# A hybrid encoder step on one core: closing sums taken place by place, and the first expert's token numbers, splits and tables in another order

## What is computed

```python
def _layer(...):
    ...
    h = _layer_norm(alpha * x + mix, ln1_g, ln1_b)
    moe_out = _moe(h.reshape(B * L, D_MODEL), w_router, b_router, w_gu, b_gu, w_down, b_down)
    y = _layer_norm(alpha * h + moe_out, ln2_g, ln2_b)

def _moe(x2, ...):
    logits = jnp.dot(x2, w_router) + b_router
    top_val, top_idx = lax.top_k(logits, TOP_K)          # 4 of 32
    gates = jax.nn.softmax(top_val, axis=-1)
    ...
    gu = jnp.dot(xb, w_gu[e]) + b_gu[e]                  # rows of one expert, 1024 x 2048
    gate, up = jnp.minimum(gu[:, :1024], 7.0), jnp.clip(gu[:, 1024:], -7.0, 7.0)
    hmid = gate * jax.nn.sigmoid(1.702 * gate) * (up + 1.0)
    out = jnp.dot(hmid, w_down[e]) + b_down[e]           # 1024 x 1024
    ...
```

## Time and profile before

| | |
|---|---|
| median of 3 runs | 1273.67 us (1271.19 to 1275.38) |
| profiled execution, its own time | 1274.26 us |
| its span | 1272.3 us |
| busy: PE, DVE, ACT, POOL | 1202.4, 1050.8, 945.9, 174.6 us |
| read from HBM, written | 452.99 MB, 29.95 MB |

### The profile page before, as it was taken

The page is one execution under the profiler, slowest core; times in us unless marked ns, Lnnn a source line. Parts: engine busy times, 40 slices in busy tenths (PEclk is TensorE's granted clock), DMA queues, the critical chain, the costliest instruction groups (busy, mean ns, idle before and its releaser), DMA issues.

```text
span 1272.3 us, 35060 instructions
## 1 busy us (share of the span) xinstructions
PE 1202.4 (95%) x15390; PEld 870.7 (68%) x15390; DVE 1050.8 (83%) x1202; ACT 945.9 (74%) x1260; POOL 174.6 (14%) x145
## 2 busy tenths in 40 slices
PE   7999998899999999999999999999999999999985
PEld 3555555677777777777777777777777777777742
DVE  6565566899988889998988888888888888888886
ACT  5433311688989888988888888888888888888821
POOL 1264210111101000100100001111111111101002
PEclk9999998899999999999999999999999999999997
DMA  9662394599999999999999999999999999999983
GB/s 364 230 246 85 108 419 164 219 363 414 426 425 424 426 425 423 425 426 426 425 426 425 424 425 425 426 425 424 424 426 424 426 424 427 424 423 427 401 351 95
DMA packets 46839, 475.00 MB, mean 373 GB/s; under 512 B 8701, under 2 KB 9620, under 8 KB 20828
## 3 DMA queue, kind: packets, MB, share of 16 engines
q1 hardware_dynamic: 34636, 438.58, 82.3%
q0 software_dynamic: 11392, 31.77, 6.6%
q10 hardware_dynamic: 656, 2.36, 0.5%
HBM read 452.99 MB, written 29.95 MB: 380 GB/s over the span
## 4 chain that ended last, share of the span: by engine, by line
PE 40%; DMA 27%; DVE 9%; issue 4%; ACT 4%; DVEq 0%; SPq 0%; ACTq 0%
PE wide L1010 28%; DMA ring<-in_w_gu 16%; PE bank L1010 11%; DMA ring<-in_w_down 8%; DVE work L1840 5%; ACT work L874 3%; DMA work<-part_rows 2%; PE bank L1319 1%; ACT work L904 1%; DVE ring L1975 1%; DVE ring L1973 1%; DVE work L1770 0%; DVE ring L1962 0%; DVE work L1831 0%; DVE work L1825 0%
## 5 line engine op out<-in xcount | busy, mean ns | idle before, releaser
L1840 DVE SCALAR_TENSOR_TENSOR work<-ring,work 128x2048 f16<-128x2048 f32 x320 | 721.3, 2287 | 108.6 <-ACT work L874 97.0
L874 ACT ACTIVATE work<-ring 128x2048 f16<-128x2048 f32 x320 | 599.6, 1902 | 86.1 <-DMA ring<-in_w_gu 60.0
L1010 PE MATMUL wide<-work 128*128 128x96 f16 (+2 forms) x7024 | 482.2, 229 | 33.9 <-DVE work L1825 8.6
L1010 PEld LDWEIGHTS wide<-work 128*128 128x128 f16 (+2 forms) x7024 | 372.2, 101 | 128.5 <-issue 44.0
L1010 PEld LDWEIGHTS bank<-work 128*128 128x128 f16 (+4 forms) x6530 | 299.2, 100 | 40.6 <-issue 26.3
L1010 PE MATMUL wide<-ring,work 128*96 128x512 f32 (+3 forms) x1004 | 326.4, 491 | 0.0
L1010 PE MATMUL bank<-work 128*128 128x96 f16 (+4 forms) x6530 | 310.0, 208 | 10.0 <-DVE work L1770 3.0
L1010 PEld LDWEIGHTS wide<-ring,work 128*96 128x96 f32 (+3 forms) x1004 | 128.6, 134 | 172.1 <-issue 122.0
L687 POOL DMA_INDIRECT work<-h_rows,work x32 | 61.3, 1916 | 463.7 <-PE bank L1319 446.5
L700 POOL DMA_INDIRECT part_rows<-work x30 | 42.7, 1422 | 371.8 <-ACT work L934 371.8
L904 ACT ACTIVATE work<-bank,work 128x96 f32<-128x96 f32 x256 | 65.1, 334 | 0.0
(11 more groups left out here) (207 smaller groups left out, 591.5 us busy)
## 6 DMA issues: line engine op xcount, KB each, us to landing
ring<-in_w_gu SPq DMA_DIRECT2D x128, 2048.0 KB, 29.2
ring<-in_w_down SPq DMA_DIRECT2D x64, 2048.0 KB, 31.9
part_rows<-work POOLq DMA_DIRECT2D x1, 10240.0 KB, 37.2
ring<-part_rows SPq DMA_DIRECT2D x3, 2560.0 KB, 26.7
ring<-in_w_in SPq DMA_DIRECT2D x3, 2048.0 KB, 13.2
ring<-in_w_out SPq DMA_DIRECT2D x2, 2048.0 KB, 10.6
h_rows<-work POOLq DMA_DIRECT2D x1, 2560.0 KB, 9.9
ring<-h_rows SPq DMA_DIRECT2D x1, 2560.0 KB, 23.4
```

Source lines behind the costliest of these rows:

```text
L874: act.activation(whi[buf(n, p)], packed(s, p), ACT.Copy, scale=W_UP).then_inc(hi_done, 1)
L1010: return pe.matmul(out, w, x, start=start, stop=stop, skip_group_check=True)
L1840: dve.scalar_tensor_tensor(wlo[buf(n, p)], packed(s, p), W_UP, whi[buf(n, p)], ALU.mult, ALU.subtract).then_inc(split_done, 1)
```

## The change

**At the start of the experts.** For expert 0 the one-hot operations are made tile by tile while tile 4 is still being ranked (`first_hot`), a product of one column brings the token numbers alone (`ids_ready`), and DVE writes `tok_i` in the middle of `gate_info(4)` (`first_ids`). POOL clears `xg` earlier. The selection of expert 0, and one-hot and table of expert 1, move behind the fourth unit of expert 0; the counts go from table 1 to table 2. `used` is made before `route(4)`. The loads of (0,4) and (0,5) move on SP behind the first gather's landing. Fillers go from 14, 8 and 12 to 9, 3, 4 and 4.

**In the close.** Each of the five numbers t becomes one piece of SBUF, `place[t]`, with five rows a partition (h and four parts), loaded by two transfers whose runs are 4 KB in place of 20 KB. The norm's weights go ahead of them on SP. DVE adds only `part` 0 (`add_first`), POOL adds `part` 1 and 2 together for t below 3, and PE adds the rest with the identity (`own`): two rows for t below 3, three for 3 and 4. Five PSUM areas in place of two. The last number's small stores go out from ACT.

```diff
+        pair = [ctx.enter_context(nc.psum_tensor(f"pair{i}", [P, 1024], F32)) for i in range(2)]
+        bank = [pair[i // 2][:, i % 2 * 512:i % 2 * 512 + 512] for i in range(4)]
...
+        def total_bank(t):
+            return (wide[0], pair[0], pair[1], wide[1], wide[0])[t]
...
-            sp.wait_ge(mix_ready, TILES)
-            for i in (4, 5):
-                load(0, i, piece_slot(0, i))
             sp.wait_ge(hT_ready, 2 * TILES)
             sp.wait_ge(h_stored, 16 * TILES)
             sp.dma_start(bguT[:, 0:E, :], b_gu).then_inc(late_in, 16)
+            sp.wait_ge(mix_ready, TILES)
             sp.wait_ge(gathered[0], 16)
+            for i in (4, 5):
+                load(0, i, piece_slot(0, i))
...
             sp.dma_start(g2n, ln2_g).then_inc(ln2_in, 16)
             sp.dma_start(b2n, ln2_b).then_inc(ln2_in, 16)
+            sp.wait_ge(scattered, 16 * (E - 2))
+            for t in range(RUN):
+                if t > 0:
+                    sp.wait_ge(split_done, PAIRS * (E - 1) + (0, 2, 6, 8, 10)[t])
+                sp.dma_start(place[t][:, 0, :], h_dram.rearrange("(p t) d -> t p d", t=RUN)[t]).then_inc(place_in[t], 16)
+                sp.dma_start(place[t][:, 1:, :], part_dram.rearrange("(j p t) d -> t p j d", j=TOPK, t=RUN)[t])\
+                  .then_inc(place_in[t], 16)
...
+            for t in range(3):
+                pool.wait_ge(place_in[t], 32)
+                pool.tensor_tensor(place[t][0:HOLD, 2, :], place[t][0:HOLD, 2, :], place[t][0:HOLD, 3, :], ALU.add)\
+                    .then_inc(middle_added, 1)
...
+            pe.wait_ge(hot_ready, 1)
+            for t in range(TILES):
+                n = ROWS[t]
+                last = mm(bank[0][:, 488:489], hot[0:n, t, :], info[0:n, t, 0, 3:4], t == 0, t == TILES - 1)
+            last.then_inc(ids_ready, 1)
+            idle(4)
...
             table(0, 0)
-            table(1, 1)
-            idle(12)
-            rows(0, 0, 16, 2)
+            idle(4)
+            rows(0, 0, 16, 1)
             for n in range(E):
                 for u in range(8):
                     unit(n, u, n % 2)
+                    if n == 0 and u == 3:
+                        pe.wait_ge(bias_ready, 1)
+                        select(0)
+                        table(1, 1)
...
+            for t in range(3):
+                first_rows(t)
+            pe.wait_ge(gates_lo, 1)
+            pe.wait_ge(last_weighed, 1)
+            for t in range(3):
+                last_rows(t)
+                pe.wait_ge(place_in[t], 32)
+                own(t, 4)
+                pe.wait_ge(middle_added, t + 1)
+                own(t, 2).then_inc(last_ready, 1)
+            for t in range(3, RUN):
+                if t == 4:
+                    pe.wait_ge(sum_sent, 1)
+                first_rows(t)
+                last_rows(t)
+                pe.wait_ge(place_in[t], 32)
+                own(t, 4)
+                own(t, 3)
+                own(t, 2).then_inc(last_ready, 1)
...
             route(TILES - 1)
+            first_hot(range(TILES - 1))
+            rank_tile(TILES - 1)
+            first_hot([TILES - 1]).then_inc(hot_ready, 1)
             gate_info(TILES - 1)
-            rank_tile(TILES - 1)
+            dve.nop().then_inc(hot_ready, 1)
...
             rows_lo(0, 0)
+            next_lo(0, 2)
+            onehot(1, 1)
+            next_lo(0, 3)
+            rows_of(1, 1, None)
             places_of(0, 0)
-            next_lo(0, 2)
-            next_lo(0, 3)
...
-            dve.wait_ge(h_in, 16)
-            add(0)
+            add_first(0)
+            add_first(1)
             dve.wait_ge(y31_high, 1)
             dve.scalar_tensor_tensor(y31_lo[0:BLK, :], wide[1][0:BLK, :], slots[(E - 1) % ROW_BUFS][:, 5:6],
                                      y31_hi[0:BLK, :], ALU.mult, ALU.subtract).then_inc(last_weighed, 1)
-            add(1)
-            add(2)
+            add_first(2)
```

More of the change, by code:

```diff
@@ L266, in build @@
         g2n, b2n = ring[:, 0:D], ring[:, D:2 * D]
[L268 to L275, removed]
+        place = [ring[:, 2 * D + t * (TOPK + 1) * D:2 * D + (t + 1) * (TOPK + 1) * D].rearrange("p (j d) -> p j d", j=TOPK + 1)
+                 for t in range(RUN)]
+        assert 2 * D + RUN * (TOPK + 1) * D <= 7 * SLOT
         x_in = [sem(f"x_in{t}") for t in range(4)]
@@ L318, in build @@
         bd_in = sem("bd_in")
-        h_in, part_in = sem("h_in"), [sem(f"part_in{j}") for j in range(TOPK)]
+        place_in, middle_added = [sem(f"place_in{t}") for t in range(RUN)], sem("middle_added")
         zeroed, tok_known = sem("zeroed"), sem("tok_known")
@@ L704, in _ @@
             gather(0, 0, 0)
+            pool.wait_ge(states_out, 96)
+            pool.wait_ge(zeroed, 32)
+            pool.iota(val_e, pattern=[[1, E], [0, MAXB - 1]], base=0, channel_multiplier=0,
+                      allow_small_or_imprecise_dtypes=True).then_inc(made, 1)
+            pool.iota(val_b, pattern=[[0, E], [BLK, MAXB - 1]], base=BLK, channel_multiplier=0,
+                      allow_small_or_imprecise_dtypes=True).then_inc(made, 1)
             gather(1, 1, 1)
@@ L728, in _ @@
                                    small[0:n, 64:65], ALU.pow).then_inc(std_ready, 1)
+            for t in range(RUN):
+                deviation(t)
         @block.scalar
@@ L1409, in half, with first_rows, last_rows, own @@
                 for c in range(2):
-                    mm(wide[t % 2][0:HOLD, c * 512:(c + 1) * 512], lhs[:, t * HOLD:(t + 1) * HOLD],
-                       rhs[:, c * 512:(c + 1) * 512], start, False)
-            def products(t):
-                if t >= 2:
-                    pe.wait_ge(sum_sent, t - 1)
+                    last = mm(total_bank(t)[0:HOLD, c * 512:(c + 1) * 512], lhs[:, t * HOLD:(t + 1) * HOLD],
+                              rhs[:, c * 512:(c + 1) * 512], start, False)
+            def first_rows(t):
                 half(t, hot30, y30_hi, True)
                 half(t, hot30, y30_lo, False)
-                if t == 0:
-                    pe.wait_ge(gates_lo, 1)
-                    pe.wait_ge(y31_high, 1)
+            def last_rows(t):
                 half(t, hot31, y31_hi, False)
-                if t == 0:
-                    pe.wait_ge(last_weighed, 1)
+                half(t, hot31[0:BLK], y31_lo[0:BLK], False)
+            def own(t, j):
                 for c in range(2):
-                    mm(wide[t % 2][0:HOLD, c * 512:(c + 1) * 512], hot31[0:BLK, t * HOLD:(t + 1) * HOLD],
-                       y31_lo[0:BLK, c * 512:(c + 1) * 512], False, False)
-            def fourth(t):
-                for c in range(2):
-                    last = mm(wide[t % 2][0:HOLD, c * 512:(c + 1) * 512], ident[0:HOLD, 0:HOLD],
-                              part[TOPK - 1][0:HOLD, t, c * 512:(c + 1) * 512], False, True)
-                last.then_inc(last_ready, 1)
+                    last = mm(total_bank(t)[0:HOLD, c * 512:(c + 1) * 512], ident[0:HOLD, 0:HOLD],
+                              place[t][0:HOLD, j, c * 512:(c + 1) * 512], False, True)
+                return last
             pe.wait_ge(up_free, 2 * E + 2)
+            pe.wait_ge(gate_free, 2 * E + 2)
             pe.wait_ge(end_hot_made, 2)
@@ L1945, in _, with add_first @@
                     hidden(b + E, 1)
-            def add(j):
-                dve.wait_ge(part_in[j], 16)
-                step(dve.tensor_tensor(yt[0:HOLD], yt[0:HOLD], part[j][0:HOLD], ALU.add))
-            dve.wait_ge(h_in, 16)
-            add(0)
+            def add_first(t):
+                dve.wait_ge(place_in[t], 32)
+                step(dve.tensor_tensor(place[t][0:HOLD, 0, :], place[t][0:HOLD, 0, :], place[t][0:HOLD, 1, :], ALU.add))
+            add_first(0)
+            add_first(1)
             dve.wait_ge(y31_high, 1)
@@ L1980, in _ @@
             for t in range(1, RUN):
+                if t >= 3:
+                    add_first(t)
                 total(t)
```

104 lines of the change are left out of this document (46 added, 58 removed).

## The result

The changed kernel takes 1286.48 us (median of four runs, 1285.32 to 1290.13) beside 1272.43 us for the kernel before on the same chip: a ratio of 1.010 (95% interval 1.0082 to 1.0119). It is 1% slower. Forecast was 1267.0 us, in a range of 1264.0 to 1272.5.

The account below looks back on a forecast made before the run. The DMA stream (425 GB/s) was taken to bound the long middle, leaving only the experts' start and the close to gain: 1.5 + 5.8 = 7.3 us off 1274.26 gave 1267.0, range 1264 to 1272.5.

Parts of the forecast that it names:

- The step that failed: Start: second gather issued near 241 in place of 238.10, with time until 253 before it delays PE.
- the 253: Start: the time in us up to which the second gather was said not to delay PE.
- Start gives back: Rival, start: deferred 4.19 MB and late loads cost 2.3 us there; 3.5 won in all, 1270.8 us; chance 0.12.
- The rival of slow places: Rival, close: PE waits for place 4; at 11.3 us a place the time is 1286; chance 0.07.
- the forecast gain: Start of the experts: 1.5 us won, range -2.3 to 2.6.
- The first split: Start: DVE's first split begins near 229.1 in place of 233.77, 4.7 us earlier.
- POOL's first gather: Start: token numbers some 2.4 us earlier, same lag to POOL, rows landing near 230.5.
- (2,1): Start: this piece can be issued near 267.1 in place of 269.93, as expert 0 ends 2.8 us earlier.
- The close: End of the kernel: 5.8 us won, the last total starting at 1256.3 in place of 1261.74.
- POOL's addition: Close: 2.5 to 4.0 us each, the upper taken; even so done before PE wants it.
- The clock: Rival, close: PE falls to half clock; one stretch costs 1.7 us, both 5.1; 1268.7 to 1272.1 us; chance 0.12.
- The 12.7 us a place: Close: a place's time by the skill's row-pitch rule; the sum would end 19 us above the time before.

Follow-up runs that it names:

- Experiments 1 to 5: Against the kernel before: new close alone 1275.46 us, new start alone 1286.29; against the changed kernel: DVE wait 1273.91, (0,4)/(0,5) loads back early 1285.75, DVE fill 1273.56.
- experiment 3: Changed kernel with one wait added: DVE goes on splitting only once POOL is past the second gather's instruction; 1273.91 us, ratio 1.0001 to the kernel before.
- experiment 9: Changed kernel with both repairs: DVE waits for POOL's second gather instruction, and y31_lo is made ahead of the second addition; 1267.10 us, ratio 0.9936 to the kernel before.
- experiment 8: New close on the old start without POOL's additions, PE adding all three rows for every number; 1278.93 us, ratio 1.0035 to the kernel before.
- experiment 7: New close on the old start, with y31_lo made ahead of the second addition; 1268.53 us, ratio 0.9957 to the kernel before.
- experiment 6: Changed kernel with pairs 4 to 7 of expert 0 scaled (one SBUF operand) and not split; 1275.95 us, ratio 1.0015 to the kernel before.
- experiment 5: Changed kernel with no wait, only a small DVE fill between places_of(0) and expert 2's one-hots; 1273.56 us, ratio 0.9992 to the kernel before.

## Why the prediction was wrong

**The step that failed** is a sentence in the part on the start: the second gather "is issued later ...; it has until 253 before it delays PE". Two things in it are wrong. The first is the instruction: it was taken to last 1 us, as it had before, and its new neighbours on DVE were not looked at. Before, it ran behind two splits and beside an operation that reads PSUM; in the new order it stands 0.4 us ahead of DVE's longest stretch of back-to-back splits. Experiments 1 to 5 show it: same place, 11.13 us with splits 0.39 or 0.40 us behind it, 1.03 and 1.05 us with splits 0.65 and 0.55 us behind, and the time of the whole kernel goes with it, by 12.6 to 12.9 us. The trace of before had a hint that I didn't read: the third gather, with a split running beside it, stood on POOL for 2.44 us, and ended 0.86 us behind that split:

```profile
257.47 2.28 DVE L1840 SCALAR_TENSOR_TENSOR work<-ring,work 128x2048 f16<-128x2048 f32 x1
...
258.17 2.44 POOL L687 DMA_INDIRECT work<-h_rows,work  x1 [19.04 <-PE bank L1319]
```

The second is the 253, which left 12 us to spare. The prediction doesn't say where it comes from; PE's transposes at 256.27 less the 3.7 us of the first gather give 252.6. But those 3.7 us were read in the standstill. With the stream running, the second gather of before took 9.9 us from issue to landing:

```profile
work<-h_rows,work POOLq DMA_INDIRECT x1, 9.9
```

In experiment 3 it took 11.7, and its rows landed 1.0 us before PE used them. So next to nothing was left to spare, and of the 10.1 us that the instruction lasted longer PE waited 9.53. Another 2.7 us came from the half clock behind that wait, which had no term.

None of the rivals was this one. "Start gives back" had its price from the stream (2.3 us), not from a gather. The rival of slow places names 1286, which is the measured time, but by chance: no place was slow.

**The start, once repaired, gives the forecast gain**: 1.6 us (0.4 to 2.8) measured, 1.5 forecast. One comparison of two profiled executions is clean, since the mixer ahead took equally long in both (to 0.3 us up to 222 us): before and experiment 9. The first split starts at 229.77 in place of 233.77, 4.0 us earlier (forecast 4.7, at 229.1), POOL's first gather 2.1 us earlier (2.4), and (2,1) is issued at 268.92 in place of 269.93, 1.0 us earlier where 2.8 was forecast. So the sum fits better than its steps, and part of the agreement is luck. In the changed kernel's own trace all this was hidden by a mixer that ended 2.2 us later; other executions have it up to 2.4 us earlier at 150 us. Rows of one execution at this place are good to 2 us.

**The close was priced on full hands.** It needed 61.6 us from the last weights on, 54.9 were forecast. The 6.7 are four terms (6.6 as rounded here): place 1 landed 0.8 later than forecast; DVE's addition took 3.40 us in place of 1.1, 2.3 more; PE's row 29.9 us in place of 26.8, 3.1 more, nearly all of it in the first twelve products (7.51 us; 4.36 in experiment 9 at full clock); and 0.4 in the tail. Two of them were in the text, in the wrong place. POOL's addition was priced (2.5 to 4.0, measured 2.34), but only as something that PE might wait for and not as something that DVE works beside. The clock was a rival with 0.12, for a wait of 1.5 us. In the kernel before it had fallen behind a longer one:

```profile
1230.76 3.34 PE L1010 MATMUL wide<-work 96*116 96x512 f16 x10 [3.68 <-DVE work L1953]
```

Here the wait was 4.88 us, long because place 1 and DVE's addition came late, and the clock fell (0.50); behind the 3.05 us of experiment 8 it didn't. So the clock's 3.1 us most likely hang on the 2.3 us of the addition, and are not a loss of their own.

**What held**: the places land 7.0, 6.4, 6.2 and 6.2 us apart (forecast 6.35), so runs of 4 KB and the 2.5 MiB between a partition's four rows cost nothing that shows, and the rival with slow places was wrong. The 12.7 us a place, which the prediction worked out from a row pitch, did not come either. PE's full-clock rates held (from `y31_lo` on its row takes 4.36 + 8.61 + 13.80 = 26.8 us in experiment 9, as forecast), and so did the order of the sums; number 4 waits for nothing. The store that went to ACT's queue won nothing: both queues issue side by side at 1284.35 and ACT's takes 0.58 and 0.31 us:

```profile
1284.35 0.32 SPq L578 DMA_DIRECT2D out<-ring  x1
1284.36 0.58 ACTq L1016 DMA_DIRECT2D out<-ring  x1
1284.97 0.31 ACTq L1018 DMA_DIRECT2D out<-ring  x1
```

The size of the close's gain was there to be had, by another order: experiment 7 is 6.1 us below the kernel before, 5.8 had been forecast. That the repaired kernel lands on the 1267.0 of the prediction is no proof of it, since one term of it needed a different order of instructions.

## What to carry to other kernels

An instruction that moves gets new neighbours, and its own time has to be read again with these: for one on POOL, look at what DVE does in the microsecond after it starts, not only at whom it waits for. A gather that POOL issues needs a head start on DVE's next long float32 operation: 0.55 us was enough here, 0.40 us was not, and a fill of 0.27 us between the two was worth 13 us. Read how long a transfer takes to land in the stretch to which it moves: 3.7 us in the standstill were 11.7 with the stream running. In a close, the operation that PE waits for goes ahead of everything on its engine that waits for a transfer, and additions that POOL and DVE make of data that landed together run one after the other.

## What the runs showed of the hardware

**POOL's gather and DVE's splits.** A gather's instruction that takes 1.0 to 1.2 us when nothing holds it was held over a stretch of DVE's float32 work: it ends 0.91 us behind the stretch in the changed kernel and in experiment 6, and 0.86 us behind a split for the third gather of the kernel before. In the first of these it missed five changes from one DVE instruction to the next, and came through at the change to short copies out of PSUM; in the last, DVE went on at once with another float32 operation of 0.55 us, and it came through all the same. What lets it in at one change and not at another stays open. The Trainium skill, "SBUF — State Buffer", section "Who interferes with whom", has VectorE and GpSimd share one pair of ports as an exclusive lock, held for a whole instruction. The traces agree that one of the two is kept out; that it is kept out over several instructions of the other is more than the section says. The section counts scalings in VectorE's faster modes among what holds GpSimd up, and experiment 6 agrees (1.23 us for a scaling, 2.28 for a split, and the gather held). Of the addition with two SBUF inputs it infers that it takes only the reading side and so leaves the making of descriptors alone. Splits have two SBUF inputs as well, and the gather's instruction took 11.13 us beside them. It also reads its token numbers from SBUF, and the section has such reads wait for an operation with two SBUF inputs; no run here tells the two apart.

**Two additions at once are one after the other.** When POOL starts first, its addition takes 2.34 us and DVE's 3.40, which is 2.34 + 1.06; when DVE starts 0.04 us ahead, its takes 1.22 and POOL's 3.38. Alone, DVE's takes 1.22 (experiment 8). Who starts first is not all: in experiment 7 POOL's addition starts at 1227.22, while `y31_lo` is being made, and DVE's at 1227.53, yet DVE's takes 1.21 us and POOL's 3.74. There too POOL was passed over at a change from one DVE instruction to the next.

**Indirect transfers** take 9 to 12 us from the end of POOL's instruction to landing while the stream runs (8.9 for the second gather of the kernel before, 10.7 in experiment 3, 11.2 in the changed kernel, 11.7 in experiment 5). From the start of the instruction it was 3.7 us in the standstill.
